# Output projections of two transformer layers: from float32 products to three float32r passes over split weights and activations

## The reference

```python
mix = jnp.concatenate([o_a, o_b, o_c], axis=-1)      # 512 tokens x 1280
x = x + mix @ w_o[l]                                 # w_o[l]: 1280 x 1024
xn = _rms_norm(x, ffn_norm[l])
gate, up = jnp.split(xn @ w_gate_up[l], 2, axis=-1)
x = x + (jax.nn.silu(gate) * up) @ w_down[l]
```

## Time and profile before

| | us |
|---|---|
| median of 3 runs (2930.11 to 2936.17) | 2935.43 |
| profiled execution, its own time | 2931.78 |
| its span | 2930.0 |
| TensorE busy, share of span | 2748.7, 94% |
| DVE, ACT, POOL busy | 1306.0, 980.5, 874.1 |
| mean granted clock of TensorE | 0.966 |

### The profile page before, as it was taken

How to read it: one execution, slowest core, us unless ns; L and a number is a source line. 1 busy time by engine, 2 the same in 40 slices (tenths; PEclk the granted TensorE clock), 3 DMA queues, 4 the chain that set the end, 5 groups by cost and what they waited for, 6 DMA issues and landing times.

```text
span 2930.0 us, 35486 instructions
## 1 busy us (share of the span) xinstructions
PE 2748.7 (94%) x13956; PEld 2132.4 (73%) x13956; DVE 1306.0 (45%) x1772; ACT 980.5 (33%) x1650; POOL 874.1 (30%) x658
## 2 busy tenths in 40 slices
PE   7988999999999799999998999898898999899998
PEld 6866658887798575788876766667776565688887
DVE  2758535543345673454424454546444212343332
ACT  5468522222243883222223443332222100122222
POOL 5566412345347552133462100300000223200000
PEclk9999999999999999999998999898997999899999
DMA  5230024545432101255452211111111332233332
GB/s 130 90 69 1 19 72 122 145 131 137 128 94 75 41 1 47 79 151 133 131 157 76 59 43 33 40 30 29 44 44 44 80 84 67 58 101 101 92 89 79
DMA packets 386102, 230.40 MB, mean 79 GB/s; under 512 B 9388, under 2 KB 382252, under 8 KB 385936
## 3 DMA queue, kind: packets, MB, share of 16 engines
q1 hardware_dynamic: 383984, 226.19, 27.9%
q0 software_dynamic: 1952, 1.94, 0.8%
HBM read 226.01 MB, written 2.10 MB: 78 GB/s over the span
## 4 chain that ended last, share of the span: by engine, by line
PE 78%; DVE 8%; ACT 7%; DMA 5%; issue 2%; POOL 0%; SPq 0%; DVEq 0%; ACTq 0%; POOLq 0%
PE ps L818 66%; PE scores L818 8%; DMA raws<-in_w_down 4%; PE ps L960 1%; DVE R L2120 1%; ACT wH L1802 1%; DVE ring_parts L2368 1%; DMA ring<-in_w_in 1%; DVE spare L2130 0%; ACT U L1641 0%; ACT R L1940 0%; DVE QK_parts L2110 0%; DVE wL L2315 0%; ACT spare L1664 0%; ACT R L1641 0%
## 5 line engine op out<-in xcount | busy, mean ns | idle before, releaser
L818 PE MATMUL ps<-xH,wH 128*128 128x512 f32 x1000 | 395.9, 396 | 6.9 <-DVE xL L2289 6.8
L818 PE MATMUL ps<-xL,wH 128*128 128x512 f32 x1000 | 390.4, 390 | 0.0
L818 PE MATMUL ps<-xH,wL 128*128 128x512 f32 x1000 | 389.9, 390 | 0.0
L1802 ACT ACTIVATE wH<-raws 128x2048 fp32r<-128x2048 f32 (+1 forms) x114 | 192.9, 1692 | 493.7 <-PE ps L818 340.2
L2315 DVE TENSOR_TENSOR wL<-raws,wH 128x2048 fp32r<-128x2048 f32 (+1 forms) x113 | 229.9, 2034 | 250.7 <-ACT wH L1802 249.8
L818 PE MATMUL ps<-ring_parts,U_parts 128*128 128x256 f32 (+1 forms) x1968 | 319.5, 291 | 23.1 <-DVE ring_parts L2172 6.2
L818 PEld LDWEIGHTS ps<-ring_parts,U_parts 128*128 128x128 f32 x1968 | 284.6, 199 | 38.4 <-issue 30.8
L818 PE MATMUL ps<-R 128*64 128x128 f32 (+6 forms) x1768 | 281.3, 348 | 28.3 <-issue 4.8
L712 POOL TENSOR_TENSOR spare<-spare,cvec 128x1024 f32<-128x1024 f32 x64 | 123.9, 1936 | 520.9 <-DMA spare<-in_w_ada 520.9
L818 PEld LDWEIGHTS ps<-R 128*64 128x64 f32 (+2 forms) x1768 | 175.0, 168 | 132.9 <-issue 77.7
L818 PE MATMUL ps<-U_parts,ring_parts 128*128 128x512 f32 (+2 forms) x720 | 216.2, 391 | 9.5 <-DVE ring_parts L2368 9.5
(11 more groups left out here) (404 smaller groups left out, 4563.5 us busy)
## 6 DMA issues: line engine op xcount, KB each, us to landing
raws<-in_w_gate_up SPq DMA_DIRECT2D x88, 512.0 KB, 5.4
ring<-in_w_in SPq DMA_DIRECT2D x34, 1024.0 KB, 5.8
spare<-in_w_ada SPq DMA_DIRECT2D x64, 512.0 KB, 3.9
raws<-in_w_down SPq DMA_DIRECT2D x32, 704.0 KB, 6.0
raws<-in_w_ffn_in SPq DMA_DIRECT2D x44, 512.0 KB, 5.0
ring<-in_w_in SPq DMA_DIRECT2D x22, 512.0 KB, 5.5
raws<-in_w_ffn_out SPq DMA_DIRECT2D x16, 704.0 KB, 4.5
ring<-in_w_o SPq DMA_DIRECT2D x6, 896.0 KB, 5.0
```

The costliest lines, as they stand in the source:

```text
L818: return nc.tensor.matmul(o, a, b, start=first, stop=last)
L1802: ap.do(f(wH[:, g % 2, 0:n], raws[:, g % 2, 0:n], ACT.Copy), wh_ready)
```

## The change

The mix is kept as two sets of tiles, `mixH` and `mixL`, and each of the eight tiles of the projection has its own piece of weights of 128 columns, in three regions of 1280 columns: raw, high, low. Four pieces lie in the ring at first (homes 0 to 3), pieces 4 and 5 take homes 0 and 1 again once tiles 0 and 1 are through, and 6 and 7 lie in regions that the scores and the values leave. ACT rounds a piece (`wo_round`), DVE subtracts (`wo_subtract`), pieces 0 and 1 in turns 39 to 42 of the attention, the others two tiles ahead of their use. The head pairs' output takes DVE two instructions instead of one, and the transposed differential outputs take ACT one and DVE one. The first two feed-forward pieces are released by tiles 4 and 5, and DVE subtracts them ahead of tiles 6 and 7.

```diff
-        mixT = [QK[:, a, :] for a in MIX_SLOTS] + [R[:, 4608 + i * S:4608 + (i + 1) * S] for i in range(3)]
+        mixH = [QKP[:, a, :] for a in MIX_SLOTS] + [parts_of_R(4608 + i * S) for i in range(3)]
+        mixL = ([QKP[:, 3, :], parts_of_R(3 * 1152 + 512), parts_of_R(6144)]
+                + [QKP[:, 8, :], parts_of_R(11904), parts_of_R(10752), parts_of_R(11264)]
+                + [parts_of_R(t * 1152 + 512) for t in range(3)])
+        WO_ROWS, WO_HOMES = 10, (0, 1, 2, 3, 0, 1, 4, 5)
+        def wo_parts(e):
+            n, home = WO_ROWS * P, WO_HOMES[e]
+            a = home * 2 * n if home < 4 else (18816, 6656)[home - 4]
+            raw_, parts_ = (ring_flat, ring_parts_flat) if home < 4 else (R, R_parts)
+            return [t.rearrange("p (k c) -> p k c", k=WO_ROWS)
+                    for t in (raw_[:, a:a + n], parts_[:, a + n:a + 2 * n], parts_[:, a:a + n])]
+        WO_SPLIT_AT = (39, 41)
...
@@ TensorE, layer(l), after the attention
-                for a, e in WO:
-                    if e < D:
-                        i = weights(3)
-                        w = slot(i, 10, e - a)
...
-                            ins = mm(bank[:, :], w[:, k, m * P:(m + 1) * P], mixT[k], n == 0, n == 9)
+                for e in range(KT):
+                    pe.wait_ge(wo_low, l * KT + e + 1)
+                    _, high, low = wo_parts(e)
+                    bank = db.fill(pe)
+                    for n, k in enumerate(MIX_ORDER):
...
+                        mm(bank[:, :], high[:, k, :], mixH[k], n == 0, False)
+                        mm(bank[:, :], high[:, k, :], mixL[k], False, False)
+                        ins = mm(bank[:, :], low[:, k, :], mixH[k], False, n == 9)
+                    ins.then_inc(d_full, 1)
+                    wo_read[l].append((d_full, db.n))
@@ SP, load_ffn(l)
-                    sp.wait_ge(*read_by[base + (before[l] - base - 1) // NSLOT * NSLOT])
+                    sp.wait_ge(*wo_read[l][4])
...
+                    if l < L and q == 1:
+                        sp.wait_ge(*wo_read[l][5])
@@ SP, per layer
-                sp.wait_ge(ot_full, (l + 1) * (N_PAIR - N_DIFF) // TT)
-                for dst, src in wo_piece(l, *WO[-1])(None):
-                    sp.dma_start(dst, src).then_inc(wo_in, 16)
+                for e in (0, 1, 2, 3, 6, 7, 4, 5):
+                    if e == 0:
+                        sp.wait_ge(*read_by[base + RING_PIECES - 2])
+                    elif e == 1:
+                        sp.wait_ge(*read_by[base + RING_PIECES - 1])
+                    elif e == 6:
+                        sp.wait_ge(s_full, (l + 1) * N_PAIR)
+                    elif e == 7:
+                        sp.wait_ge(ot_full, (l + 1) * (N_PAIR - N_DIFF) // TT)
+                    elif e in (4, 5):
+                        sp.wait_ge(*wo_read[l][e - 4])
+                    for dst, src in wo_dmas(l, e):
+                        sp.dma_start(dst, src).then_inc(wo_in[WO_HOMES[e]], 16)
@@ ACT, attention
-                        ap.do(f(mixT[3 + i], D_BANKS[1][:, :], ACT.Copy), mix_done)
+                        ap.do(f(mixH[3 + i], D_BANKS[1][:, :], ACT.Copy), mix_high)
+                    if p_ in WO_SPLIT_AT:
+                        wo_round(l, WO_SPLIT_AT.index(p_))
+
+            def wo_round(l, e):
+                raw_, high, _ = wo_parts(e)
+                act.wait_ge(*wo_landed(l, e))
+                ap.do(f(high, raw_, ACT.Copy), wo_high)
@@ ACT, tiles
                 for k in range(KT):
+                    if k + 2 < KT:
+                        wo_round(l, k + 2)
+                    else:
+                        split_high(l, k + 2 - KT)
                     high_tile(xH[:, k, :], k)
                     square_in_turn(k)
-                    if k >= 5 and k < 7:
-                        split_high(l, k - 5)
@@ DVE, attention
-                    vp.do(v.tensor_copy(mixT[(7, 8, 9, 0, 1, 2)[n]], D_BANKS[0][:, :]), ot_done)
+                    k = (7, 8, 9, 0, 1, 2)[n]
+                    vp.do(v.tensor_copy(mixH[k], D_BANKS[0][:, :]))
+                    vp.do(v.tensor_tensor(mixL[k], D_BANKS[0][:, :], mixH[k].bitcast(F32), ALU.subtract), ot_done)
+                def diff_output_low(i):
+                    dve.wait_ge(mix_high, l * BH + i + 1)
+                    vp.do(v.tensor_tensor(mixL[3 + i], D_BANKS[1][:, :], mixH[3 + i].bitcast(F32), ALU.subtract), mix_done)
...
+            def wo_subtract(l, e):
+                raw_, high, low_ = wo_parts(e)
+                dve.wait_ge(wo_high, l * KT + e + 1)
+                vp.do(v.tensor_tensor(low_, raw_, high.bitcast(F32), ALU.subtract), wo_low)
@@ DVE, tiles
                 for m in range(KT):
+                    if m + 2 < KT:
+                        wo_subtract(l, m + 2)
+                    else:
+                        split_low(l, m + 2 - KT)
                     bank = db.take(dve)
...
-                    if m == 6:
-                        split_low(l, 0)
                     fold(m)
-                split_low(l, 1)
```

More of the change, by code:

```diff
@@ L374, in build @@
         gate_full, gate_scaled = sem("gate_full"), sem("gate_scaled")
-        wo_in = sem("wo_in")
+        wo_in = [sem(f"wo_in{i}") for i in range(6)]
+        wo_high, wo_low, mix_high = sem("wo_high"), sem("wo_low"), sem("mix_high")
+        wo_read = [[], []]
         root_ready = sem("root_ready")
@@ L430, in build @@
         c1 = c0 + RD
-        WO = [(0, 256), (256, 512), (512, 768), (768, 1024)]
         HK = FT // 2
@@ L462, in piece_parts, with wo_dmas, wo_landed @@
             return [ring_parts[:, i, o:o + KT * n].rearrange("p (k c) -> p k c", k=KT) for o in (h, 0)]
[L464 to L472, removed]
+        def wo_dmas(l, e):
+            w, c_ = wo_parts(e)[0], slice(e * P, (e + 1) * P)
+            yield w[:, 0:7, :], cols(A["w_o"][l], e * P, (e + 1) * P)[:, 0:7, :]
+            for c in range(2):
+                r = VG + c * GH // 2 * GD
+                yield w[c * GD:(c + 1) * GD, 7:10, :], A["w_o"][l][r:r + GH // 2 * GD, c_].rearrange("(i p) c -> p i c", p=GD)
+        def wo_landed(l, e):
+            home = WO_HOMES[e]
+            return wo_in[home], 48 * (l * WO_HOMES.count(home) + WO_HOMES[:e + 1].count(home))
         def layer_pieces(l):
@@ L1085, in layer @@
                 run(attention)
-                for a, e in WO:
-                    if e < D:
-                        i = weights(3)
-                        w = slot(i, 10, e - a)
[L1091 to L1099, removed]
-                                pe.wait_ge(ot_done, l * (GH + AH) // 2 + {7: 3, 0: 5, 2: 6}[k])
-                            ins = mm(bank[:, :], w[:, k, m * P:(m + 1) * P], mixT[k], n == 0, n == 9)
-                        ins.then_inc(d_full, 1)
-                    if e < D:
-                        read_by.append((d_full, db.n))
+                for e in range(KT):
[3 more added lines that the diff above has]
+                    for n, k in enumerate(MIX_ORDER):
+                        if e == 0 and k == MIX_ORDER[0]:
+                            pe.wait_ge(mix_done, (l + 1) * BH)
+                        if e == 0 and k in (7, 0, 2):
+                            pe.wait_ge(ot_done, l * (GH + AH) // 2 + {7: 3, 0: 5, 2: 6}[k])
+                        mm(bank[:, :], high[:, k, :], mixH[k], n == 0, False)
[3 more added lines that the diff above has]
+                    wo_read[l].append((d_full, db.n))
                 ffn(l)
```

16 lines of the change are left out of this document (10 added, 6 removed).

## The result

The changed kernel takes 2913.23 us (median of 4 runs, 2910.89 to 2914.77), the kernel before 2935.22 in the same comparison: ratio 0.9917, 95% interval 0.9900 to 0.9934. It is 22 us faster; 23.6 were forecast (2911.8). The profiled execution took 2910.89 us with a span of 2909.0, against 2930.0: 20.98 less.

What follows compares the result with a forecast made beforehand. The prediction took TensorE alone to bound the output tiles. Per layer, -13.9 us from products and +2.1 in the attention gave -11.8, in all -23.6: 2911.8 us as a median, range 2903 to 2924.

Steps and rivals of the forecast that it cites:

- The products, -13.9 us per layer: Output tiles: 240 float32r instructions at 0.2271 us replace 80 float32 products, 54.5 us instead of 68.37 per layer.
- half of a float32 record (0.2137): Output tiles: lower bound on time per product, 51.3 us per layer; as the plain quarter rival 2905.4 us, chance 0.07.
- Splits, 0: Weight splits in the tiles: DVE about 5.0 us of a 6.81 us tile, hidden behind TensorE, 0 us.
- rival that the split chain becomes the bound: Output tiles: DVE at 7.3 us a tile exceeds TensorE; +8 to +12 us, 2920 to 2924 us; chance 0.06.
- Loads, 0: Weight loads: 24 DMAs per layer instead of 12, all in time; second feed-forward piece about 4 us early; 0 us.
- The 1.4 of slack: Second feed-forward piece: slack counted behind its about 4 us till ACT's turn, before lateness costs TensorE time.
- The attention, +2.1 us per layer: Head pairs: second DVE operation adds 0.72 us before freeing the bank; third shows 0.65, fourth and fifth 0.72, others 0.
- The rival of the clock in the longer gap: Fifth head pair: TensorE's wait grows to 1.95 us and the clock falls; +3.3 us, 2915.1 us; chance 0.18.
- A low clock at the attention's tail: Sign of a wrong forecast: granted clock under 1.00 at the attention's tail or in the tiles.
- Tile 7's low part, 0 with 1.5 us of slack left: Last output tile: low part some 0.2 us late against 1.69 us of earlier slack; 0 us.
- The sum: Whole kernel: -11.8 us per layer, -23.6 in all; profiled execution 2908.2 us, median 3.65 above it at 2911.8.

Runs made afterwards that it cites:

- the second copy alone: Kernel before the change, with each of six head pairs' banks copied twice by VectorE, only the second copy freeing the bank: 2939.47 us, ratio 1.0002.
- the trace compared first: Profiled execution of the changed kernel in its first comparison with the kernel before, also called the first trace: 2910.89 us; that comparison's median 2913.23 us.
- the second trace: The changed kernel run once more, unaltered, on the next run's chip as a yardstick: 2912.97 us, ratio 0.9918 to the kernel before.
- the experiment: Changed kernel with GpSimd's multiplication for the conditioning weights held back until the feed-forward's first bank is full: 2906.36 us, one execution.
- these 14 traces: Traces of all kernels in the study, two layers each, counted together for clock falls; no single time.

## Why the prediction was right

- **The products, -13.9 us per layer:** -13.83, at 0.2273 us against 0.2271. The feed-forward's own row was the right source; half of a float32 record (0.2137) would have promised 3.2 us more per layer. The Trainium skill's 215.7 ns (TensorE: Matmul & The Clock Gate, "Wait — 56ns, not 53.3ns?") gives, as an estimate, 2.8 us more per layer; the trace decides against it for these products, with 227.3 ns.
- **Splits, 0:** right. VectorE's whole turn is 5.65 us, not 5.0: my sum held its first wait for ScalarE (0.83) and not the second (0.56). So the room was 1.17 us a tile where I had 1.8 (6.81 - 5.0). The rival that the split chain becomes the bound needed VectorE's 4.05 busy us of a turn to grow by 29%; with GpSimd idle they did not.
- **Loads, 0:** right; the second piece had 4.2 us to spare before its subtraction was late, with "about 4 us" counted. The 1.4 of slack counted behind that was not there: GpSimd had taken it (tile 7's low part, below).
- **The attention, +2.1 us per layer:** the one term mis-sized. Alone it measured 2.64 and 2.61 us. The step that failed is "the first comes while ACT is busy 15.30 of 16 us and TensorE gets its time from ACT; both 0". The first pair cost 0.57 us: its wait grew by 0.73, and from the scores before it (282.76, 283.95 after) to the product behind the 2.4 us wait it is 18.22 us instead of 17.64 (18.21 with the second copy alone). The trace of before had said so in a line that the prediction did not read: TensorE already waited 0.34 us for VectorE's copy there. ScalarE's busy share was no cover: ScalarE came 0.57 us later to its table load itself (85.76 us into the attention, 85.19 before), and the 2.40 us wait stayed 2.39. The second pair and the sixth show no wait, the third cost 0.58 (0.65 said), the fourth 0.72, the fifth 0.62. These make 2.49 of the 2.71; the last 0.2 I can't place.
- **The rival of the clock in the longer gap:** its price per fall was right (1.65 us said, 1.7 measured), its certainty not. Behind 1.84 to 1.96 us the clock fell in 6 of 14 layers, in the trace compared first in none; in four of the six no fall had come behind the 2.4 us wait, and the layer was no slower for it. A low clock at the attention's tail was one of the prediction's signs of being wrong, and the second trace has it. The same kind of event, behind the wait of 2.4 us that both kernels have, added 1.4 us to layer 1 in the first trace.
- **Tile 7's low part, 0 with 1.5 us of slack left:** wrong by the side I did not look at, and its wait was another of the signs of being wrong. VectorE subtracts the first feed-forward piece ahead of tile 6's addition, so it is done at 404.05 instead of 417.50. SyncE, which waits for that before it loads the third piece and behind it the conditioning's weights, issues the latter at 405.12 instead of 418.57, and GpSimd's first multiplication moved from after the tiles (425.06) to 411.52, beside tile 7's gain. Price: 0.22 us of wait, 0.5 us per layer by the experiment.
- **The sum:** -27.7 from the tiles, +6.9 from the attentions, +0.1 from the first groups, -0.4 in the rest. The forecast had -27.8 and +4.2. Against the profiled execution it is 2.7 us off (2910.89 for 2908.2), nearly all of it the attentions, and of that 1.5 the long low stretch. The median stands 2.3 us above that execution instead of the 3.65 assumed, which leaves 1.4: that this part of the miss cancels is luck.

## What to carry to other kernels

Take the price of a product from the same form elsewhere in the same trace, and check a new helper's load by the engine's whole turn with its waits, not by its busy time. Where one instruction that frees a buffer becomes two, look at each place for an existing wait with that releaser: there the second is paid nearly in full (0.57 to 0.72 of 0.72 us here), whatever other engine seems busy, and the cheap remedy is to move the pair ahead of its neighbour in the queue. Judge edits of a few us by stages cut at the same events: here a total moved by 18 us in code that nobody touched, at a lower granted clock. Where the same stage differs between executions, look for VectorE instructions that began beside one of GpSimd's.

## What was not expected of the hardware

- After a wait of TensorE, 1.2 GHz is a matter of odds in these 14 traces: 0 of 12 at 1.08 to 1.23 us, 6 of 14 at 1.84 to 1.96, 21 of 26 at 2.4, 2 of 2 at 2.57; one stretch costs 1.7 us, a long one 1.4 more.
- VectorE on SBUF operands is held up by GpSimd: 0.49 to 1.68 us (TENSOR_SCALAR, 128x512), 0.75 to 1.92 (SCALAR_TENSOR_TENSOR, 128x512). It is no slowing in proportion: the held one ends a fixed time behind the GpSimd instruction, 0.55 us for the second and 0.27 for the gain (413.70, and 411.52 + 1.91 = 413.43), so the delay is what was left of GpSimd's. The low part (L2308) took 0.88 instead of 0.69. The 128x512 copies and subtractions out of PSUM took 0.69 us each in the attentions of all 14 traces, beside GpSimd or not.
